# Where the activation rows of a two-block transformer kernel lie in SBUF: rows 1024 bytes apart, high and low parts at one address modulo 256

## The reference, cut to what matters

```python
def swiglu(x, w_gu, w_down):
    g, u = jnp.split(x @ w_gu, 2, axis=-1)
    return (jax.nn.silu(g) * u) @ w_down
...
h = h + 0.5 * swiglu(rmsnorm(h, ffn1_norm[i]), ffn1_w_gu[i], ffn1_w_down[i])
u = rmsnorm(h, mix_norm[i])
b_g, c_g, v_c, q_c, kv_c, k_r, g_conv, g_mla = jnp.split(u @ w_in[i], split_pts, axis=-1)
...
gate = jax.nn.sigmoid(rmsnorm(h, ple_norm[i]) @ w_ple_gate[i])
```

## The kernel before, in words

| tile | offsets of the high rows | offsets of the low rows |
|---|---|---|
| xh, xl; gh, gl | 0, 16, ... 112 | 128, 144, ... 240 |
| hh, hl | 0, 16 (even steps), 32, 48 (odd steps) | 64, 80; 96, 112 |
| mh, ml and the other tiles of the mixer in `ra` | 0 | 0 |

## Time and profile before

### The profile page before, as it was taken

How to read it: one execution, slowest core, us unless ns; L and a number is a source line. 1 busy time by engine, 2 the same in 40 slices (tenths; PEclk the granted TensorE clock), 3 DMA queues, 4 the chain that set the end, 5 groups by cost and what they waited for, 6 DMA issues and landing times.

```text
span 1978.2 us, 36952 instructions
## 1 busy us (share of the span) xinstructions
PE 1935.2 (98%) x16060; PEld 1916.9 (97%) x16060; DVE 1350.9 (68%) x1608; ACT 996.9 (50%) x1233; POOL 237.4 (12%) x168
## 2 busy tenths in 40 slices
PE   8999999999999999999999999998999999899999
PEld 8999999999999999999999999898999999799998
DVE  6655777775559655687785557896855589676556
ACT  5443545563437444545554445776533466654443
POOL 3000100010002000100010001473100016710000
PEclk9999999999999999999999999999999999899999
DMA  8555454465554655544556554424555543237551
GB/s 278 199 180 182 144 174 160 133 211 192 192 183 156 213 182 183 183 137 143 171 171 213 185 181 152 158 67 132 170 187 187 166 152 113 70 112 231 191 183 53
DMA packets 246533, 329.57 MB, mean 167 GB/s; under 512 B 6246, under 2 KB 218788, under 8 KB 246372
## 3 DMA queue, kind: packets, MB, share of 16 engines
q1 hardware_dynamic: 246018, 326.79, 50.0%
q0 software_dynamic: 96, 0.26, 0.1%
q10 hardware_dynamic: 258, 0.16, 0.0%
HBM read 326.14 MB, written 1.05 MB: 165 GB/s over the span
## 4 chain that ended last, share of the span: by engine, by line
PE 79%; DVE 12%; POOL 3%; ACT 3%; DMA 1%; issue 1%; SPq 0%; POOLq 0%; DVEq 0%; ACTq 0%
PE work L2028 17%; PE work L2029 17%; PE work L2030 17%; PE acc L2028 9%; PE acc L2030 9%; PE acc L2029 9%; DVE w_lo L1313 4%; POOL fa L747 2%; ACT w_hi L800 1%; DVE ra L1326 1%; DMA raw<-in_w_in_dram 1%; DVE xl L1347 1%; DVE fa L1358 1%; POOL fa L741 1%; PE acc L2105 1%
## 5 line engine op out<-in xcount | busy, mean ns | idle before, releaser
L1313 DVE TENSOR_TENSOR w_lo<-raw,w_hi 128x2048 fp32r<-128x2048 f32 (+2 forms) x313 | 709.8, 2271 | 107.8 <-ACT w_hi L800 105.8
L2028 PE MATMUL work<-xh,w_hi 128*128 128x256 f32 x2560 | 721.8, 282 | 9.6 <-DVE w_lo L1313 6.1
L2029 PE MATMUL work<-xl,w_hi 128*128 128x256 f32 x2560 | 718.6, 281 | 0.0
L2030 PE MATMUL work<-xh,w_lo 128*128 128x256 f32 x2560 | 717.0, 280 | 0.0
L800 ACT ACTIVATE w_hi<-raw 128x2048 fp32r<-128x2048 f32 (+2 forms) x313 | 576.6, 1849 | 165.4 <-PE work L2030 74.6
L2028 PEld LDWEIGHTS work<-xh,w_hi 128*128 128x128 f32 x2560 | 482.3, 188 | 13.9 <-issue 8.0
L2029 PEld LDWEIGHTS work<-xl,w_hi 128*128 128x128 f32 x2560 | 483.0, 189 | 0.3
L2030 PEld LDWEIGHTS work<-xh,w_lo 128*128 128x128 f32 x2560 | 483.1, 189 | 0.0
L2028 PE MATMUL acc<-ra,w_hi 128*128 128x256 f32 x1352 | 380.1, 281 | 0.0
L2030 PE MATMUL acc<-ra,w_lo 128*128 128x256 f32 x1352 | 379.7, 281 | 0.0
L2029 PE MATMUL acc<-ra,w_hi 128*128 128x256 f32 x1352 | 378.9, 280 | 0.0
(11 more groups left out here) (302 smaller groups left out, 2324.7 us busy)
## 6 DMA issues: line engine op xcount, KB each, us to landing
raw<-in_ffn_w_gu_dram SPq DMA_DIRECT2D x88, 1024.0 KB, 5.1
raw<-in_w_in_dram SPq DMA_DIRECT2D x52, 1024.0 KB, 5.5
raw<-in_ffn_w_down_dram SPq DMA_DIRECT2D x44, 1024.0 KB, 4.9
raw<-in_w_up_dram SPq DMA_DIRECT2D x32, 1024.0 KB, 5.3
raw<-in_w_down_dram SPq DMA_DIRECT2D x32, 1024.0 KB, 4.9
raw<-in_w_mla_out_dram SPq DMA_DIRECT2D x8, 1024.0 KB, 5.5
raw<-in_w_o_dram SPq DMA_DIRECT2D x8, 1024.0 KB, 4.9
raw<-in_w_ple_gate_dram SPq DMA_DIRECT2D x8, 1024.0 KB, 5.0
```

The source lines that it names most:

```text
L1313: v.tensor_tensor(w_lo[:, s, 0:n], raw[:, r, 0:n], w_hi[:, s, 0:n].bitcast(F32), ALU.subtract).then_inc(lo_done.sem, 1)
L2028: pe.matmul(dst, ah, bh, start=start and i == 0, stop=False, skip_group_check=not group)
L2029: pe.matmul(dst, ah, bl, start=False, stop=False, skip_group_check=not group)
L2030: last = pe.matmul(dst, al, bh, start=False, stop=stop and i == len(pairs) - 1, skip_group_check=not group)
```

## The change

The eight rows of `xh` and of `xl` become slices of one tensor `x_rows` of 4160 elements, as large as the two before, so nothing behind it moves. Rows of all three pairs are 256 elements (1024 bytes) apart, and the start of each tile is set by hand: `xh` and `xl` at elements 16 and 2064 of `x_rows`, `hh` and `hl` at 32 and 1056 of `ra`, `gh` and `gl` at 4168 and 6216 of `ra`. Offsets become: 64 for all rows of `xh` and `xl`, 128 for all of `hh` and `hl`, 32 for all of `gh` and `gl`. No instruction is added, removed or moved, and no size, wait or transfer changes.

```diff
-ROW = T + 4
+X_SIZE, X_ROW, X_AT = 4160, 256, (16, 2064)
+H_ROW, H_AT = 256, (32, 1056)
+G_ROW, G_AT = 256, (4168, 6216)
...
-        xh = sb("xh", [P, KD, ROW], F32R)[:, :, 0:T]
-        xl = sb("xl", [P, KD, ROW], F32R)[:, :, 0:T]
+        x_rows = sb("x_rows", [P, X_SIZE], F32R)
...
+        def rows_at(arena, at, n, row):
+
+            return cut(arena, at, n, row)[:, :, 0:T]
+
+        xh, xl = (rows_at(x_rows, at, KD, X_ROW) for at in X_AT)
...
-        hh, hl = (cut(ra, i * 4 * ROW, 2, 2, ROW)[:, :, :, 0:T] for i in range(2))
+        hh, hl = (rows_at(ra, at, 4, H_ROW).rearrange("p (a b) t -> p a b t", a=2) for at in H_AT)
...
-        gh, gl = (cut(ra, 4 * ROW * 4 + i * KD * ROW, KD, ROW)[:, :, 0:T] for i in range(2))
+        gh, gl = (rows_at(ra, at, KD, G_ROW) for at in G_AT)
```

## The result

The changed kernel takes 1982.07 us (median of 20 runs, 1979.67 to 1984.13), the kernel before 1979.5 us in as many runs beside it (1977.26 to 1981.98). The ratio is 1.0015, with a 95% interval of 1.0008 to 1.0022: slower by 1.6 to 4.4 us, at the median less than the 0.2% (4 us) that the forecast called a difference. The forecast of 1971 us was 11 us too low, and its sign was wrong. One of the executions of the kernel before, beside the last but one batch of experiments, took 6283 us and is in no ratio.

A forecast was written before the change was run, and what follows sets the result against it. The prediction took TensorE's gapless matmul stream to bound the kernel; x rows -6.5, inner tile +0.7 and gate -0.6 us sum to -6.4, giving 1971 us, with an 8 in 10 range of 1941 to 2000.

The forecast's parts named there:

- What bounds the kernel: Feed-forward steps: TensorE's matmuls follow without gap, 16.94 to 16.98 us a step; VectorE has 2.8 us or more to spare.
- x rows: 8064 matmuls on x, all at offset 64 after: 117.5 to 116.7 ns each, -6.5 us; ends -33.9 and +20.2.
- the two pure paces: Matmuls meeting one address start on beats of 6.67 ns: 18 beats (120.0 ns) or 17 (113.3); an estimate.
- The sum over parts: Whole kernel: every term a count times a difference in pace; -6.5 + 0.7 - 0.6 = -6.4 us.
- Inner tile: 3648 matmuls in feed-forward layers, 118.1 ns to the 118.3 of `dots`: +0.7 us; ends -17.5 and +6.9.
- Gate: 768 matmuls in four layers, 117.5 ns before, at offset 32 the value taken for 64: -0.6 us; ends -3.2, +1.9.
- x as the stationary operand: `by_token`, 672 matmuls whose weights come to one offset; 1 ns either way is 0.7 us; taken as nothing.
- The long beat: Rival, `product` on x: every matmul waits as at offset 0, 120.0 ns, up to +20.2 us, 2000 us; chance 0.33.
- The short beat: Rival, x and gate: offset 64 locks at 113.3 ns, -33.9 and -3.2 us, 1941 us; chance 0.18.
- no address matters: Rival, all tiles: overlap of two reads costs the same at every offset, terms near zero, 1977.5 us; chance 0.15.
- The signs to look for: Profile after: 48 on x 5.60 us, starts repeating after one or two matmuls, inner tile 5.68 in both steps, mixer 1.44.
- The rule that was weighed: Skill page on TensorE: two independent ports and 109 ns for 256 columns; by these the change would do nothing.

The follow-up runs named there:

- x alone: Against the changed kernel, inner tile and gate go back to their stepping rows, x stays at offset 64: 1972.31 us, ratio 0.9963 to the kernel before.
- the two kernels at 192 with another `X_SIZE`: Against the changed kernel, x, inner tile and gate at 192; `x_rows` 64 bytes longer (mixer's rows at 64): 1945.02 us; 64 bytes shorter (mixer at 192): 1935.56 us.
- the kernel with 0: Against the changed kernel, rows of x, inner tile and gate all at offset 0: 2004.07 us, ratio 1.0119 to the kernel before.
- 0/16: Against x at 64 with gate stepping, both inner steps have high rows at 0 and 16, low at 64 and 80: 1981.91 us, ratio 1.0016.
- all_192: Against the changed kernel, rows of x, inner tile and gate all at offset 192: 1967.14 us, ratio 0.9936 to the kernel before.

## Why the prediction was wrong

**What bounds the kernel.** Right. Three steps of the feed-forward follow TensorE's pace and nothing else, before, after, and in every experiment, and behind the openings of the feed-forward layers no distance between starts is above 130 ns in any trace; a faster pace reached the time nearly in full (9.1 us of fast stretches against 9.8 us between the times of x alone and of the change), and VectorE never became late in these steps, even at 16.56 us. That the address has a hand in the pace was right too: 120.0 at offset 0 on every tile, 24 us in all. That it sets the pace alone was wrong.

**x rows: the step that failed.** "For 64 I take the middle of the two pure paces, 17.5 beats, 116.7". Measured: 117.8 in nearly all stretches of the change. The term was -6.5 us and came out as +0.8. The pure pace of 17 beats does exist at 64, 113.4 with its first steps in 28 stretches of the kernel with x alone, but 18 was not seen, nor a mixture of the two: the other state is a rhythm of its own, 117.78. In the 62 stretches of the change, once settled, single distances are 117 to 119 and never 113 or 120, and any three in a row are 353 or 354 ns: 53 beats over three matmuls, 53 x 6.67 = 353.3. The middle of the two pure paces is one that no steady stretch at 64 has. It does exist elsewhere, at offset 32 (the gate's 5.60 us above), so the beat was a fair guess and the choice among its values was not one that the rows could make. The sum that the beat was read from could not have shown it either: 2.82 us, a difference of two times read to 0.01 us, can't be told from 422 or 424 beats.

**The sum over parts.** The prediction priced each tile by its own offset and added up. This is the deeper error. x alone would have borne the forecast out by accident (1972.3 against 1971.5), since 2112 of its 8064 matmuls on x run fast; the inner tile at 128, priced at +0.7 us, took those 9.1 us away by the rhythm in which it hands over. The whole can't be had from the parts' terms.

**Inner tile.** 118.3 taken from `dots`, 118.6 to 118.7 measured; +0.7 against +1.3 us with the gate's share in it. The row of `dots` was read to 0.01 us in 1.42, which can't tell 118.3 from 118.7: the precision of the row was the limit, and `dots` itself has 118.4 in means over its starts, entry steps included; once settled it goes through the same five distances as the inner tile after the change (119, 115, 118, 122, 120), so it was a fair model.

**Gate.** -0.6 us; measured -0.1 to -0.2 (117.75 to 117.47 over 768). Right in sign and within the bounds, but by luck: most of three layers became slower, 117.8, and the third ran at 116.7.

**x as the stationary operand.** Taken as nothing, with 0.7 us for 1 ns. It gained 2.5 ns in the mean, -1.4 us, since half of its stretches ran at 113.4 to 113.8: the largest gain that the change made, in the term that was left out. It also shows that the address of the moving operand is not what counts by itself: the columns that move there lie where they lay, and only the stationary rows moved. `dots` says the same from the other side: with all of its tiles moved by 64 bytes together (the two kernels at 192 with another `X_SIZE`) its settled distances stay at 119, 115, 118, 122, 120 within 2 ns.

**The rivals.** The long beat stood for the slower side at 0.33 with 120.0; the sign came from near it, but the size from a state that no rival had. "It decides the sign as soon as the pace at 64 is above 117.5" held, with 117.8. The short beat appeared on x in one stretch of 48 in the mixer, in part of one `pair` and in two twelves of the output projection, and for whole layers' worth in five other kernels. That no address matters is excluded by the kernel with 0. The range of 1941 to 2000 held 1982.

**The signs to look for.** 5.60 us for 48 on x was 5.65. "Repeat after one or two matmuls" was wrong: sums over three matmuls on x are alike to 1 ns, and sums over nine are 1059 to 1061 ns in the first feed-forward layer; the inner tile's distances come back after five (119, 115, 118, 122, 120). Only offset 0 has one distance, 120. Even and odd steps of the inner tile did become alike, the mixer stayed, and busy times of VectorE and ScalarE did.

**The rule that was weighed.** The Trainium skill, TensorE: Matmul & The Clock Gate, gives two independent ports in Part 2 and 109 ns under Back-to-back issue gap. The section gives that formula for an isolated matmul and says that in a stream of pairs of weight load and matmul both set the spacing, so the forecast set a stream against a figure that is not for streams. No stretch of matmuls of 256 columns in any run here has 109; the fastest steady pace is 113.3, the slowest 120.0, and with nothing but addresses changed the pace moves between them. The measurement decides against one pace for every address in this stream; whether it is the reading of the weights that the running matmul loses time to, no run shows.

**Not settled.** Why an offset has the rhythms that it has, and by what a wait or a row of another offset changes one into the other. A start's history matters, that is shown; a mechanism in the memory is not. Nor was it seen whether the fast rhythm at 64 would last through a layer if all its rows lay there: that kernel had it in the opening `pair` of the last feed-forward layer, for some 70 matmuls, and was in the slow one behind the wait of 1.3 us that followed. Of the +2.6 us of the change some 0.7 are paces in the profiled pair; the rest is in distances with waits and was not taken apart by an experiment, though the kernel with 0/16 shares it (+0.2 in paces, +2.8 in span) and x alone does not (-8.4 and -8.0). The clock goes with part of it. In the kernel before, 22 executions of the three batches with a mean granted clock of 0.995 or 0.996 have a median of 1978.5 us and 12 at 0.991 to 0.993 one of 1981.0; the change has its median of 1982.8 in 13 executions at 0.991 to 0.993, and at 0.994 it has 1981.1 (six) against 1980.1 (eight). At like clock the change is then 1 to 2 us slower, an estimate from these executions. Whether the layout makes the lower clock more frequent was not tried.

## What to carry to other kernels

Where a stream of matmuls with a weight load each leaves no gap, its pace depends on where the moving row lies against the weights, by 6% here; try layouts with all moving tiles at one offset (192 for all of them gave 2.2%, 144 for three of them lost 0.5%), and keep offset 0 out. Price a layout as a whole and over several executions: a stretch can have two stable paces at one address, the stretch ahead picks between them, and changes of single tiles neither add up nor say what the full layout does. An average over a mixed pattern says nothing of its members: read single stretches before taking a mean for a pace, and do not put the middle of two locked states where one of them has to be chosen.

## What the runs showed of the hardware that was not expected

**Locked paces.** At full clock, steady paces of 256-column matmuls with a weight load each: 120.0 ns at offset 0; 117.8 or 113.3 at 64 and 192; 117.8 or 116.7 at 32; 118.7 at 128, and 120.0 in a group of `dots` at 128 in the three executions of all_192, as 118, 120, 122 or within 1 ns of it; 118.7, 116.7 or 113.3 at 144; 118.6 or 117.3 at 160; 119.2, 119.1, 118.3 and 117.2 at 176, 208, 224 and 240. In units of 6.67 ns these are 18, 17.67, 17, 17.8, 17.5 and so on: whole counts over one to five matmuls for the ones seen most. The estimate of a beat fits these sums; that each start falls on one does not for the others than 120.0 and 113.3, whose single distances (117 to 119, say) are no whole counts.

**A clock stretch of some microseconds.** In the last attention the granted clock falls to 0.5, that is 1.2 of 2.4 GHz. Windows of 4 us, of the kernel after:

```profile
1694.00:1698.00 4.00, 4.00 (x33) 3.72 (x33) 3.52 (x11) 2.93 (x11) 3.71 (x4) 1.00 0.02 4
1698.00:1702.00 4.00, 2.84 (x20) 2.67 (x20) 3.97 (x7) 3.74 (x12) 3.92 (x2) 0.79 0.00 0
1702.00:1706.00 4.00, 4.00 (x21) 4.00 (x21) 0.72 (x3) 3.76 (x10) 3.66 (x4) 0.50 0.22 66
1706.00:1710.00 4.00, 4.00 (x20) 4.00 (x20) 3.95 (x5) 2.18 (x8) 3.44 (x4) 0.50 0.00 0
```

and of the kernel before, which at this place has one such window instead of two and a half:

```profile
1694.00:1698.00 4.00, 3.16 (x28) 2.84 (x26) 3.91 (x5) 2.89 (x12) 3.86 (x3) 1.00 0.00 0
1698.00:1702.00 4.00, 3.52 (x17) 3.55 (x18) 2.02 (x7) 2.87 (x5) 3.78 (x3) 0.58 0.19 66
1702.00:1706.00 4.00, 4.00 (x35) 4.00 (x36) 2.93 (x5) 3.95 (x14) 3.63 (x5) 0.99 0.00 0
```

TensorE had gaps in the window of the fall or the one ahead, in both. The kernel after has some 20 matmuls in a window at 0.5 where it has 33 in one at 1.00. Its lag behind the kernel before grew from 2.8 to 5.4 us through this stretch, but fell back to 2.2 at the next wait, where both wait for other engines, so that little of it reaches the end. The kernel with x alone changed had no fall at this place at all (its next one began at 1711 us, where TensorE stood idle for some 4 us), and the one with 0/16 the same as the change. Which of them falls was not taken further.
